# Weight remainders on VectorE alone, and a norm's squares summed on GpSimd before TensorE takes the mean

## The reference, cut to what matters

```python
# first block, for i in range(2)
h = rms_norm(x, norm_g[i])
z = h @ w_in[i]                       # three mixers read columns of z
x = x + y @ w_out[i]
gate = jax.nn.sigmoid(rms_norm(x, ple_norm_g[i]) @ ple_w_gate[i])
x = x + gate * (p[i] @ ple_w_proj[i])
# then rms_norm(x, final_norm_g)
# second block, for l in range(2)
h = rms_norm_2(x, attn_norm[l])       # l = 0: nsa_mixer, l = 1: forgetting_attention
o_mem = memory_attention(q_mem, mem, mem_norm[l], w_mem_kv[l])
x = x + jnp.concatenate([o_mix, o_mem], axis=-1) @ w_o[l]
u = rms_norm_2(x, ffn_norm[l]) @ w_up[l]          # 2 x 2816 columns
u = conv3(u) + conv_b                              # per channel, over 3 tokens
x = x + (silu(a) * b) @ w_down[l]                  # a, b: the halves of u
# rms_norm: x * rsqrt(mean(x * x) + eps) * g
```

## Time and profile before

| | |
|---|---|
| time, median of 3 runs | 1552.84 us (1551.9 to 1553.16) |
| the profiled execution: its own time, span | 1553.33 us, 1551.4 us |
| mean granted TensorE clock | 0.853 |
| PE busy | 1340.0 us, 86% |
| DVE busy | 897.6 us, 58% |
| ACT busy | 648.6 us, 42% |
| POOL busy | 495.3 us, 32% |
| chain that ended last, by engine | PE 37%, DVE 16%, ACT 7%, issue 2% |
| DMA | 167.56 MB, mean 108 GB/s |

### The profile page before, as it was taken

How to read it: one execution, slowest core, us unless ns; L and a number is a source line. 1 busy time by engine, 2 the same in 40 slices (tenths; PEclk the granted TensorE clock), 3 DMA queues, 4 the chain that set the end, 5 groups by cost and what they waited for, 6 DMA issues and landing times.

```text
span 1551.4 us, 25100 instructions
## 1 busy us (share of the span) xinstructions
PE 1340.0 (86%) x10545; PEld 1223.1 (79%) x10545; DVE 897.6 (58%) x1579; ACT 648.6 (42%) x1144; POOL 495.3 (32%) x294
## 2 busy tenths in 40 slices
PE   3969885989698859879899899986988999999787
PEld 3957774988577749779777699885988878999787
DVE  1884647457746474557755446777436344588842
ACT  3533123465331235554532345454434333555541
POOL 1544100334440003346400224444545201344541
PEclk9989966999799659889855599998989856999989
DMA  6324100344330004326210144443534301444450
GB/s 242 133 102 141 56 2 1 114 159 136 109 131 29 2 1 169 130 82 234 73 55 1 44 147 136 136 154 131 182 132 139 132 1 55 139 161 163 153 179 35
DMA packets 24448, 167.56 MB, mean 108 GB/s; under 512 B 2704, under 2 KB 2832, under 8 KB 8336
## 3 DMA queue, kind: packets, MB, share of 16 engines
q1 hardware_dynamic: 24336, 165.96, 30.8%
HBM read 164.90 MB, written 1.05 MB: 107 GB/s over the span
## 4 chain that ended last, share of the span: by engine, by line
PE 37%; DVE 16%; ACT 7%; issue 2%; POOL 0%; DMA 0%; DVEq 0%; ACTq 0%; SPq 0%
PE ps L445 7%; PE ps L440 7%; PE ps L442 7%; DVE ARENA L2038 5%; PE ps L603 4%; PE ps L622 4%; DVE FR L399 3%; ACT FR L386 3%; DVE WL L399 2%; ACT WH L386 2%; PE ps L612 2%; DVE ARENA L2030 1%; PE ps L483 1%; PE ps L471 1%; PE ps L463 1%
## 5 line engine op out<-in xcount | busy, mean ns | idle before, releaser
L399 POOL TENSOR_TENSOR WL<-raw,WH 128x1024 fp32r<-128x1024 f32 (+3 forms) x105 | 246.6, 2349 | 385.4 <-ACT WH L386 385.3
L440 PE MATMUL ps<-FR,WH 128*128 128x256 f32 x1156 | 290.8, 290 | 43.4 <-ACT WH L386 28.8
L442 PE MATMUL ps<-FR,WH 128*128 128x256 f32 x1156 | 285.0, 285 | 2.3 <-DVE FR L504 1.3
L440 PEld LDWEIGHTS ps<-FR,WH 128*128 128x128 f32 x1156 | 222.5, 192 | 47.5 <-issue 31.9
L386 ACT ACTIVATE WH<-raw 128x1024 fp32r<-128x1024 f32 (+4 forms) x211 | 203.1, 984 | 132.6 <-PE ps L445 68.1
L399 DVE TENSOR_TENSOR WL<-raw,WH 128x1024 fp32r<-128x1024 f32 (+4 forms) x106 | 155.0, 1464 | 156.1 <-ACT WH L386 156.0
L440 PE MATMUL ps<-FR,FR 128*128 128x256 f32 x772 | 201.0, 296 | 30.1 <-ACT FR L508 22.9
L442 PEld LDWEIGHTS ps<-FR,WH 128*128 128x128 f32 x1156 | 222.5, 192 | 4.3 <-DVE FR L504 2.0
L442 PE MATMUL ps<-FR,FR 128*128 128x256 f32 x772 | 198.8, 292 | 4.3 <-DVE FR L512 3.7
L399 POOL TENSOR_TENSOR FR<-raw,FR 128x1024 fp32r<-128x1024 f32 (+2 forms) x58 | 141.4, 2441 | 137.7 <-ACT FR L386 137.7
L440 PEld LDWEIGHTS ps<-FR,FR 128*128 128x128 f32 x772 | 152.6, 198 | 35.5 <-ACT FR L508 21.5
(11 more groups left out here) (315 smaller groups left out, 2147.4 us busy)
## 6 DMA issues: line engine op xcount, KB each, us to landing
raw<-wst_in SPq DMA_DIRECT2D x123, 1024.0 KB, 4.9
raw<-wst_in SPq DMA_DIRECT2D x17, 896.0 KB, 4.6
raw<-wst_in SPq DMA_DIRECT2D x11, 768.0 KB, 4.3
raw<-wst_in SPq DMA_DIRECT2D x4, 912.0 KB, 4.6
cst<-cst_in SPq DMA_DIRECT2D x1, 1681.0 KB, 13.3
X<-xT_in SPq DMA_DIRECT2D x2, 512.0 KB, 4.4
ARENA<-memT_in SPq DMA_DIRECT2D x1, 1024.0 KB, 4.8
out_dram<-X SPq DMA_DIRECT2D x2, 512.0 KB, 2.6
```

Of the source, the lines that this page charges most:

```text
L399: e.tensor_tensor(lo[:, 0:cols], src, hi[:, 0:cols].bitcast(F32), SUB).then_inc(*put(LO[me], ("lo", i)))
L440: pe.matmul(out, hv[:, k, :], src.hi[:, c, :], start=k0 == 0 and k == ks[0], stop=False)
L442: pe.matmul(out, hv[:, k, :], src.lo[:, c, :], start=False, stop=False)
```

## The change

Two edits go together.

First, `split_lo` exists for VectorE alone: it computes the remainder of every item. GpSimd's calls of `split_lo` are gone. It had 163 of the 325 remainders in the profile (105 to WL, 58 to FR).

Second, GpSimd gets `sum_squares`: it adds the four pairs of squared chunks into one pair, three additions of 128x512 for a norm, each as soon as the next square is there. TensorE's `mean_mm` then does two matmuls for a norm instead of eight, and is called once. In "w_out", "w_o" and "down" the calls between the output pairs are gone; the one call stands after the first products of the next stage, at the start of "fox", and after the last FFN. The squares of these stages have three buffers instead of two, and only ScalarE's last square of a norm waits, for the first addition.

```diff
-    nxt = {"A": 0, "V": 0, "G": 0}
-    def lo_engine(i):
-        return "V" if i % 2 == 0 else "G"
+    nxt = {"A": 0, "V": 0}
...
-    def split_lo(e, q, me, *event, ahead=None):
+    def split_lo(v, q, *event, ahead=None):
...
-            if not split or lo_engine(i) != me:
+            if not split:
                 continue
...
-            e.tensor_tensor(lo[:, 0:cols], src, hi[:, 0:cols].bitcast(F32), SUB).then_inc(*put(LO[me], ("lo", i)))
+            v.tensor_tensor(lo[:, 0:cols], src, hi[:, 0:cols].bitcast(F32), SUB).then_inc(*put("split_lo", ("lo", i)))
...
-    def mean_mm(tag, c0, sq):
-        qpe.wait_ge(*got("square", tag, c0))
-        if c0 == 0 and B.mean_before:
+    def mean_mm(tag, sq):
+        qpe.wait_ge(*got("summed", tag, 6))
+        if B.mean_before:
             qpe.wait_ge(*got("mean free", B.mean_before))
         for c in range(2):
-            ins = pe.matmul(mean_bank[:, 0:S], C("mean"), sq[:, c, :], start=c0 + c == 0, stop=c0 + c == 7)
+            ins = pe.matmul(mean_bank[:, 0:S], C("mean"), sq[:, c, :], start=c == 0, stop=c == 1)
...
+    def sum_squares(g_, q, tag, sq, steps=(1, 2, 3)):
+        for n in steps:
+            q.wait_ge(*got("square", tag, 2 * n))
+            if n > 1:
+                q.wait_ge(*own("square_sum"))
+            g_.tensor_tensor(sq[0], sq[0], sq[n], ADD).then_inc(*put("square_sum", ("summed", tag, 2 * n)))
...
+    def three_squares(m):
+        a, b, c = m.some(3, 512, "p (c t) -> p c t", c=2)
+        return a, b, c, b
...
 # ScalarE in w_out; alike in w_o and down
-            if c0 >= 4:
-                q.wait_ge(*got("mean", ("out", l), c0 - 4))
-            a.activation(m.sq2[(c0 // 2) % 2], X[:, c0:c0 + 2, :], ACT.Square)
+            if c0 == 6:
+                q.wait_ge(*got("summed", ("out", l), 2))
+            a.activation(m.sq2[c0 // 2], X[:, c0:c0 + 2, :], ACT.Square)
...
 # GpSimd at the end of a layer of the first block
-        for c0 in range(0, 8, 2):
-            split_lo(g_, q, "G", "w_out", l, c0)
-        for c0 in range(0, 8, 2):
-            split_lo(g_, q, "G", "w_gate", l, c0)
-            split_lo(g_, q, "G", "w_proj", l, c0)
+        sum_squares(g_, q, ("out", l), lo_[l].sq2)
+        if l == 1:
+            sum_squares(g_, q, "mem", mem_sq)
+        sum_squares(g_, q, ("in", l + 1), lo_[l].sq3)
         if l == 1:
             for i in range(2):
                 scaled_g(g_, q, mem_parts[i], ("mem", i), mem_hs)
```

More of the change, by code:

```diff
@@ L514, in rstd_a @@
     def rstd_a(a, q, tag, y):
-        q.wait_ge(*got("mean", tag, 6))
+        q.wait_ge(*got("mean", tag))
         table(a, LNEXP)
@@ L1406, in layer_pe @@
                 if c0 == 0:
-                    for c in (range(0, 8, 2) if l == 0 else (4, 6)):
-                        mean_mm(("in", l), c, m.sq[c // 2] if l == 0 else lo_[0].sq3[c // 2])
+                    mean_mm(("in", l), m.sq[0] if l == 0 else lo_[0].sq3[0])
             elif s[0] == "gate":
@@ L1471, in layer_v @@
                 c0 = 2 * s[1]
-                split_lo(v, q, "V", "cols", l, c0)
+                split_lo(v, q, "cols", l, c0)
                 if c0 == 0:
@@ L1661, in layer_g @@
             barrier(q, "G", ("O", 0))
+        else:
+            sum_squares(g_, q, ("in", 0), m.sq)
         for s in SCRIPT:
@@ L1733, in out_pe @@
                      "w_proj", l, c0, kc=2)
-            if c0 >= 4 and l == 0:
-                mean_mm(("in", 1), c0 - 4, m.sq3[c0 // 2 - 2])
             if l == 1 and c0 == 2:
                 ps = begin_bank("mem mean")
-                for c in range(8):
-                    if c % 2 == 0:
-                        qpe.wait_ge(*got("mem sq", c))
-                    ins = pe.matmul(ps[:, 0:S], C("mean"), mem_sq[c // 2][:, c % 2, :], start=c == 0, stop=c == 7)
+                qpe.wait_ge(*got("summed", "mem", 6))
+                for c in range(2):
+                    ins = pe.matmul(ps[:, 0:S], C("mean"), mem_sq[0][:, c, :], start=c == 0, stop=c == 1)
                 ins.then_inc(*put("mem_pe", ("mem mean",)))
@@ L1812, in out_a @@
                     for c in range(0, 8, 2):
-                        a.activation(mem_sq[c // 2], M[:, c:c + 2, :], ACT.Square).then_inc(*put("mem_a", ("mem sq", c)))
+                        a.activation(mem_sq[c // 2], M[:, c:c + 2, :], ACT.Square).then_inc(*put("square", ("square", "mem", c)))
             if l == 1 and c0 == 4:
@@ L1883, in between_pe @@
     def between_pe():
-        for c in range(0, 8, 2):
-            mean_mm(("in", 2), c, lo_[1].sq3[c // 2])
+        mean_mm(("in", 2), lo_[1].sq3[0])
         memory_kv_pe(0)
-        for c in range(0, 8, 2):
-            mean_mm(("fin", 1), c, t_sq[c // 2])
+        mean_mm(("fin", 1), t_sq[0])
         B.mark("PE", "end", "T", "PE")
@@ L1952, in o_v @@
         barrier(q, "V", stage)
-        split_lo(v, q, "V", "w_o", l, 0, ahead=5)
+        split_lo(v, q, "w_o", l, 0, ahead=5)
         for c in range(8):
@@ L1957, in o_v @@
         for c0 in range(0, 8, 2):
-            split_lo(v, q, "V", "w_o", l, c0)
+            split_lo(v, q, "w_o", l, c0)
             ps, free = psum("w_o", l, c0)
@@ L1980, in o_a @@
                 part_x_hi(a, m.H, ("HF", l), c, vcol("ffn_norm_2", l, 0, 8))
-            if c0 >= 4:
-                q.wait_ge(*got("mean", ("o", l), c0 - 4))
-            a.activation(m.sq[(c0 // 2) % 2], X[:, c0:c0 + 2, :], ACT.Square).then_inc(*put("square", ("square", ("o", l), c0)))
+            if c0 == 6:
+                q.wait_ge(*got("summed", ("o", l), 2))
+            a.activation(m.sq[c0 // 2], X[:, c0:c0 + 2, :], ACT.Square).then_inc(*put("square", ("square", ("o", l), c0)))
         B.mark("A", "end", ("P", l), "A")
     def o_g(g_, q, l):
-        for c0 in range(0, 8, 2):
-            split_lo(g_, q, "G", "w_o", l, c0)
+        sum_squares(g_, q, ("o", l), om[l].sq)
         B.mark("G", "end", ("P", l), "G")
@@ L2081, in ffn_a @@
             q.wait_ge(*got("x f", l, c0))
-            if c0 >= 4:
-                q.wait_ge(*got("mean", ("f", l), c0 - 4))
-            a.activation(m.sq[(c0 // 2) % 2], X[:, c0:c0 + 2, :], ACT.Square).then_inc(*put("square", ("square", ("f", l), c0)))
+            if c0 == 6:
+                q.wait_ge(*got("summed", ("f", l), 2))
+            a.activation(m.sq[c0 // 2], X[:, c0:c0 + 2, :], ACT.Square).then_inc(*put("square", ("square", ("f", l), c0)))
         B.mark("A", "end", ("F", l), "A")
@@ L2100, in ffn_g @@
                 g_.tensor_tensor(m.fb[n % 3], u[0], u[1], MUL).then_inc(*put("ffn_g", ("f", l, n)))
-        for c0 in range(0, 8, 2):
-            split_lo(g_, q, "G", "down", l, c0)
+        sum_squares(g_, q, ("f", l), fm[l].sq)
         B.mark("G", "end", ("F", l), "G")
```

98 lines of the change are left out of this document (33 added, 65 removed), and 4 rows, old and new, of the table SEMS.

## The result

The changed kernel takes 1510.36 us (median of 4 runs, 1508.77 to 1511.41) against 1552.37 for the one before in the same series. The ratio is 0.9728, with an interval from 0.9712 to 0.9745: 42 us faster. The forecast was 1501, 9 us too low. The profiled execution has a span of 1509.5 (1551.4 before) and a clock of 0.849.

What follows compares the result with a forecast made beforehand. A ring through ScalarE and VectorE, stretched where VectorE and GpSimd take turns on SBUF, bounds the up steps. Terms sum to -51.9 from the profiled 1553.33, giving 1501.4, as a median 1501; range 1490 to 1512, chance 0.58.

Steps and rivals of the forecast that it cites:

- The up steps: Both FFNs: steps fall from 7.26 and 6.52 to 6.1, giving -24 and -8.4 us.
- the ring: FFN up steps: ScalarE's `hi` copies, VectorE's remainders, evacuation, taps, ScalarE's activation, `hi` again; 6.08 after the change.
- Cols: First block's layers: the mixers' chain loses waits behind GpSimd; -3.3 a layer, -6.6 in all, ends 0 and -12.
- The first norm: Kernel's first norm: two mean matmuls instead of eight save 2.6 where TensorE is the pace.
- the additions hold VectorE: Rival: each of 33 GpSimd additions can stop VectorE up to 1.29, 43 in all, giving 1544; chance 0.03.
- w_o: First: additions to X 6.57 apart fall to 5.95, -1.9; second: three mean calls go, -2.0.
- "Rows" and attention of layer 1: VectorE's 3.43 idle before the evacuation hides a second remainder of 1.13; attention has no remainders: 0.
- The gate stages: First block: line 1752 stands behind added remainders, +1.13 or more in four pairs; +2.8 first layer, +2.2 second.
- The second layer's end: Memory's low parts wait behind three additions, +2.4; with "between", means, gate stage and waits that go, -3.4.
- "Down" of the first FFN: Three removed mean calls save 2.0, the norm's end waits +1.4 for an addition: -0.6.
- The smaller gain: Rival: the up steps' cycle stays at 6.5 and the layers give nothing: 1525; chance 0.20.
- Slower: Rival: VectorE must finish two remainders before each evacuation, TensorE waits for the bank: +34, 1587; chance 0.06.

Runs made afterwards that it cites:

- e3: The kernel before with only the odd remainders of the FFN's up products moved to VectorE; 1522.81 us, ratio 0.9809.
- e4: The changed kernel with only the odd remainders of the FFN's up products put back on GpSimd; 1545.47 us, ratio 0.9955.
- e5: The kernel before, with GpSimd computing only 8 of 1024 columns of its remainders of the FFN's up products; 1506.45 us, ratio 0.9704.
- e6: The kernel before, with GpSimd writing zeros instead of computing its remainders of the FFN's up products; 1506.51 us, ratio 0.9707.
- e7: The changed kernel with VectorE's evacuation (line 2020) ahead of the two remainders in the FFN's up steps; 1488.52 us, ratio 0.9593.
- e1: The kernel before with every remainder on VectorE, means as before (eight matmuls, no additions on GpSimd); 1516.36 us, ratio 0.9758.
- e8: The changed kernel with half of VectorE's gate-stage remainders behind the evacuation at line 1751 instead of ahead; 1504.98 us, ratio 0.9696.
- e9: The changed kernel with e7's and e8's edits, four matmuls for each FFN's last norm, eight for the norm behind layer 2; 1478.91 us, ratio 0.953.
- e12: Against the kernel before: remainders on VectorE with e7's and e8's order, means by eight matmuls, no additions on GpSimd; 1495.62 us, ratio 0.9637.

## Why the prediction was right, and where it missed

**The up steps: right in mechanism and size.** The steps are 6.09 where the ring gave 6.08, and the two FFNs gave 24.1 and 7.6 for 24 and 8.4. e3 and e4 show that this gain hangs on these remainders alone, e5 and e6 that it is GpSimd's read beside VectorE that had stretched them, and e7 that the ring set the pace and not TensorE.

**"Cols": right in size, by luck in its parts.** I had 1.9 from the last taps and 1.4 from short waits. The wait before TensorE's matmul fell only from 13.27 to 12.39, and the other 2.3 of the 3.2 come before it. A remainder now stands ahead of the last tap, behind an operation of GpSimd that isn't a remainder. VectorE, then GpSimd:

```profile
93.04 2.82 DVE L395 TENSOR_TENSOR WL<-raw,WH 128x1024 fp32r<-128x1024 f32 x1
```

```profile
92.34 2.45 POOL L1354 TENSOR_TENSOR ARENA<-ARENA 128x768 f32<-128x768 f32 x1 [5.59 <-DVE ARENA L1212]
```

GpSimd's ends at 94.79, the remainder 1.07 later: it stood still as in the earlier trace rows.

**The first norm: -2.6 forecast, -0.65 measured.** The removed matmuls are gone, but here the rival "the additions hold VectorE" came true. Timeline of GpSimd and VectorE at the start of the changed kernel:

```profile
25.83 2.68 POOL L489 TENSOR_TENSOR ARENA<-ARENA 128x512 f32<-128x512 f32 x2 [2.80 <-ACT ARENA L1597]
26.18 2.61 DVE L507 SCALAR_TENSOR_TENSOR FR<-X,vec,FR 128x256 fp32r<-128x256 f32 x2 [0.37 <-ACT FR L503]
```

Two low parts that take 0.88 take 2.61, and three remainders queue behind them, done at 32.20. In e1, without additions, they are done at 30.49. How the 0.65 divides can't be read: the kernel before and three that do the same up to here (e3, e5, e6) reach the norm at 37.00 to 37.96, the changed kernel and six that do the same as it at 36.35 to 37.82. Elsewhere, too, additions stop VectorE: beside 24 of the 33, one of its operations takes 0.25 to 1.1 longer than the shortest of its form, some 13 us in all where the rival had 43. How much of this costs time wasn't measured; in "w_o" it costs none, since TensorE's pace decides there all the same.

**"w_o": near in size, for another reason.** I had taken the first "w_o" for VectorE's pace, with 0.5 a step for the addition in front of the remainder, and nothing for the means. The additions to X are 5.65 to 5.76 apart; TensorE's pace decides. e1, with the means as before, stands at 26.38 between the kernel before (27.13) and the changed one (24.60): the remainders gave 0.75 and the three removed calls 1.8, as they did in the second "w_o".

**"Rows" and attention of layer 1: 0 forecast, +2.6 measured, and not by any edit.** No instruction waits for the added remainders there. TensorE did the same matmuls at another clock; the section on the hardware has the rows. This step of mine, that equal work takes equal time, failed. Even so the one trace of the kernel before is not a fixed mark: e3, e5 and e6, the same up to there, take 174.0 to 174.2 where it has 176.7.

**The gate stages: mechanism right, size small.** +3.8 in the first instead of +2.8. I had counted one remainder of 1024 columns a pair, partly hidden; the one of 256 and TensorE's own waits for small remainders come on top. e1, without additions, has 41.84 in the first as well, so it is the remainders'. e8 gives it back in layer 1.

**The second layer's end: -3.4 forecast, -0.5 measured.** I had +2.4 for the memory's low parts behind the additions, less 0.8; it was +3.9 from the middle of the gate stage to the norm. GpSimd in the changed kernel, then in e9, which has no addition there:

```profile
646.74 2.67 POOL L489 TENSOR_TENSOR ARENA<-ARENA 128x512 f32<-128x512 f32 x2
649.37 4.21 POOL L515 TENSOR_TENSOR FR<-ARENA,FR 128x256 fp32r<-128x256 f32 x5
```

```profile
640.48 3.32 POOL L539 TENSOR_TENSOR FR<-ARENA,FR 128x256 fp32r<-128x256 f32 x4 [26.72 <-ACT FR L535]
```

In e9 that stretch is 26.68 long, 30.76 in the changed kernel, 26.89 before. e9 has e8's order as well, so it doesn't tell the two causes apart; e1 does, with the remainders on VectorE and no additions: 27.88. So the additions cost 2.9 and the remainders 1.0. The rest of what was missing: "w_out" gave 1.5 for 2.0, the "fin" norm 2.2 for 2.6, and the stretch between the norm behind "w_out" and the memory's norm step only 0.7.

**"Down" of the first FFN: -0.6 forecast, +1.0 measured.** The added wait is as priced. TensorE's mean in the changed kernel waits for the addition:

```profile
1113.06 1.13 PE L479 MATMUL ps<-ARENA,cst 128*128 128x256 f32 x4 [2.85 <-POOL ARENA L489]
```

From the square at 1111.04 to it are 2.02, against 0.68 before: +1.34 for my +1.4. The -2.0 of the three removed calls came to -0.3. From the last evacuation of the up steps to the second addition to X, TensorE has as many matmuls as before (214 records for 213), and they took 34.2 instead of 33.1; the mean clock of the first of these two stretches was 0.66 instead of 0.73.

**NSA and fox.** NSA gained 3.1 instead of 1.0. e1 has the same gain (209.7, with 212.7 before and 209.6 after) and e3 doesn't (212.6), so it is that of the remainders outside the up steps; which waits carry it wasn't followed. Fox lost 1.3 instead of gaining 0.8, which is within the spread of the same work (under the table of the kernels). Its remainders do gain, but ScalarE's next copies then wait for the weights. Waits of the changed kernel around it:

```profile
ACT WH L382 <- DMA raw<-wst_in: 2.4, 1, 2.4
ACT FR L382 <- DMA raw<-wst_in: 1.9, 1, 1.9
```

Before, these are 2.1 and 1.0. The transfer is what is late next. How much of the 2 us this is, against the clock of the same stretch (0.87 for 0.94), stays open.

**The rivals.** The smaller gain (1525) had its mechanism wrong: the ring did reach 6.1. What was lost lay in the small stages, in part in "rows", where nothing was changed that anyone waits for. "Slower" would have needed VectorE late at the evacuations; in "rows" it is not.

**The signs.** The steps are at 6.1, the additions at 1.34, and the matmuls of the means fell from 88 to 22. (These are ten norms of X and the memory's, eleven in all and not twelve, so 66 matmuls go.) Two signs missed: two remainders of the changed kernel take 2.82, where no row of 2.5 was to be left, since GpSimd still has operations of its own beside them; and the gate stage is 3.8 longer instead of 1 to 3.

## What to carry to other kernels

An instruction that takes twice its usual time, with nothing to wait for, has a neighbour on another engine: look for the row whose end plus the usual time is its own end, and price the ring without it. Moving all work of a kind to one engine can shorten both, when they had taken turns; put what others wait for (the evacuation) ahead of it in the queue. A second edit may be worth nothing until the first has emptied the engine it uses: the means alone cost 11 us, on top of the remainders they gave 6, and 17 with the orders mended and the means' own two late places repaired (e9 against e12).
